# A convolution on TensorE in four 64x64 tiles, and a new order of the steps around it

## The reference

```python
def conformer_conv(a, b, w_dw, b_dw, ln_g, ln_b):      # 512 channels, kernel 31
    u = a * jax.nn.sigmoid(b)
    y = lax.conv_general_dilated(
        u, w_dw[:, None, :], window_strides=(1,), padding=[(CONV_KERNEL - 1, 0)],
        dimension_numbers=('NWC', 'WIO', 'NWC'), feature_group_count=CONV_WIDTH)
    y = layernorm(y + b_dw, ln_g, ln_b)
    return jax.nn.silu(y)

def nsa_mixer(q, k_c, v_c, k_s, v_s, k_w, v_w, gate_logits, positions, ...):
    ...      # three attentions of 8 heads: compressed, selected and window keys
    out = g[..., 0:1] * o_cmp + g[..., 1:2] * o_slc + g[..., 2:3] * o_win

proj = hn @ w_in[l]
...
h = h + jnp.concatenate([y_conv, y_nsa], axis=-1) @ w_out[l]
```

## Time and profile before

| of the profiled execution | |
|---|---|
| span, and time | 1634.1 us; the runs' median is 1633.84 us |
| PE busy | 1572.9 us, 96% |
| PEld busy | 1437.0 us, 88% |
| DVE busy | 1188.7 us, 73% |
| ACT busy | 861.1 us, 53% |
| POOL busy | 351.8 us, 22% |
| chain of waits | PE 80%, DVE 11%, ACT 4%, issue 2%, POOL 1% |
| DMA | 271.15 MB, mean 166 GB/s |

### The profile page before, as it was taken

How to read it: one execution, slowest core, us unless ns; L and a number is a source line. 1 busy time by engine, 2 the same in 40 slices (tenths; PEclk the granted TensorE clock), 3 DMA queues, 4 the chain that set the end, 5 groups by cost and what they waited for, 6 DMA issues and landing times.

```text
span 1634.1 us, 31405 instructions
## 1 busy us (share of the span) xinstructions
PE 1572.9 (96%) x10490; PEld 1437.0 (88%) x10490; DVE 1188.7 (73%) x2258; ACT 861.1 (53%) x1587; POOL 351.8 (22%) x260
## 2 busy tenths in 40 slices
PE   8899998999999999999999999999999999999997
PEld 8789987999887887898999999988888999999996
DVE  3788676788756678455579678779998767776776
ACT  5564445655556643565554555554444545444544
POOL 2344332011000422122048755540000000000000
PEclk9899999999999999999999999999999999999999
DMA  7333244555564720154546644457777665555654
GB/s 268 126 103 104 91 142 155 171 162 180 188 194 126 234 76 1 42 191 142 168 150 203 201 149 145 136 184 241 241 241 227 201 183 190 182 190 183 189 186 148
DMA packets 87848, 271.15 MB, mean 166 GB/s; under 512 B 9824, under 2 KB 26336, under 8 KB 87392
## 3 DMA queue, kind: packets, MB, share of 16 engines
q1 hardware_dynamic: 65088, 237.01, 45.2%
q10 hardware_dynamic: 22688, 33.16, 6.2%
HBM read 258.60 MB, written 11.53 MB: 165 GB/s over the span
## 4 chain that ended last, share of the span: by engine, by line
PE 80%; DVE 11%; ACT 4%; issue 2%; POOL 1%; ACTq 1%; DMA 0%; DVEq 0%; POOLq 0%
PE ps_chunk L488 42%; PE ps_misc L488 21%; PE ps_misc L295 7%; PE ps_chunk L295 4%; PE ps_misc L2457 4%; DVE ffn_arena L1584 1%; DVE w_lo L428 1%; ACT w_hi L421 1%; PE ps_misc L798 1%; DVE mixers_arena L2257 1%; DVE mixers_arena L2258 1%; DVE mixers_arena L2254 1%; PE ps_chunk L495 1%; POOL w_lo L428 1%; DVE mixers_arena L2253 1%
## 5 line engine op out<-in xcount | busy, mean ns | idle before, releaser
L421 ACT ACTIVATE w_hi<-raw 128x512 fp32r<-128x512 f32 (+1 forms) x900 | 548.5, 626 | 495.2 <-PE ps_chunk L488 292.0
L428 DVE TENSOR_TENSOR w_lo<-raw,w_hi 128x512 fp32r<-128x512 f32 x671 | 490.1, 745 | 269.1 <-ACT w_hi L421 259.4
L488 PE MATMUL ps_chunk<-x_hi,w_hi 128*128 128x256 f32 x1792 | 520.0, 290 | 13.6 <-DVE w_lo L428 7.3
L488 PE MATMUL ps_chunk<-x_hi,w_lo 128*128 128x256 f32 x1792 | 508.6, 284 | 0.0
L488 PE MATMUL ps_chunk<-x_lo,w_hi 128*128 128x256 f32 x1792 | 508.3, 284 | 0.0
L428 POOL TENSOR_TENSOR w_lo<-raw,w_hi 128x512 fp32r<-128x512 f32 (+2 forms) x229 | 299.8, 1323 | 539.3 <-ACT w_hi L421 476.0
L488 PEld LDWEIGHTS ps_chunk<-x_hi,w_hi 128*128 128x128 f32 x1792 | 344.8, 192 | 26.1 <-POOL w_lo L428 10.2
L488 PEld LDWEIGHTS ps_chunk<-x_hi,w_lo 128*128 128x128 f32 x1792 | 345.0, 193 | 3.2 <-issue 0.5
L488 PEld LDWEIGHTS ps_chunk<-x_lo,w_hi 128*128 128x128 f32 x1792 | 344.8, 192 | 0.0
L488 PE MATMUL ps_misc<-w_hi,hid_hi 128*128 128x512 f32 x520 | 203.5, 391 | 2.1 <-DVE hid_lo L2536 1.4
L488 PE MATMUL ps_misc<-w_hi,hid_lo 128*128 128x512 f32 x520 | 203.1, 391 | 0.0
(11 more groups left out here) (342 smaller groups left out, 1795.4 us busy)
## 6 DMA issues: line engine op xcount, KB each, us to landing
raw<-in_stream SPq DMA_DIRECT2D x452, 512.0 KB, 3.6
early_rows<-row ACTq DMA_DIRECT2D x64, 128.0 KB, 1.7
row<-early_rows ACTq DMA_DIRECT2D x62, 128.0 KB, 3.2
memory_kv<-mixers_arena ACTq DMA_DIRECT2D x4, 512.0 KB, 5.2
mixers_arena<-in_cmp_w ACTq DMA_DIRECT2D x1, 2048.0 KB, 7.7
mixers_arena<-memory_kv ACTq DMA_DIRECT2D x4, 512.0 KB, 6.3
mixers_arena<-in_consts ACTq DMA_DIRECT2D x1, 1729.0 KB, 7.9
row<-in_rows ACTq DMA_DIRECT2D x3, 512.0 KB, 6.6
```

What stands on the lines that cost most here:

```text
L421: e.activation(w_hi[q % 2][:, s], raw[q][:, s], ACT.Copy).then_inc(made, 1)
L428: e.tensor_tensor(w_lo[q % 2][:, s], raw[q][:, s], w_hi[q % 2][:, s].bitcast(F32), ALU.subtract).then_inc(made, 1)
L488: last = e.matmul(o, stationary[a], moving[b], start=start and i == 0, stop=stop and i == 2, skip_group_check=True)
```

## The change

Three things change, all in the second mixers.

First, the diagonals. A diagonal of 128 channels becomes two of 64x64, each at its own quarter of the array: two groups of channels are taken together (a pair), and for each tap there are four matmuls of 64 rows by 64 columns with 256 time steps, one for each combination of row half and column half. Two of the four write their own half of the channels straight, the other two swapped (row half 0 to column half 1). Each pair takes two PSUM banks, and the strand's bank range grows from two banks (2, 2) to four (0, 4), shared with the dense product. POOL makes one 64-column eye out of the identity and then four builds of 1280 elements instead of eight. The result comes back in eight DVE adds of 64 partitions instead of four of 128.

Second, the DVE taps keep their running sums in Y in SBUF instead of PSUM bank 0, with the bias put in by the first one.

Third, `tile` has a further `yield` behind the turns of the compressed round and behind those of every other round, and MIXERS_2_ORDER is a new string.

```diff
@@ MIXERS_2_ORDER @@
-MIXERS_2_ORDER = ("ddqddddddkddqqddddddddddddddkdddddddddkdddddddqddddddqdddddqqddkddqdqkkkkddqdkdkdddkkccddkdddddddkkk"
...
+MIXERS_2_ORDER = ("ddddddddddddddddkddddddddddddddddddddqdqqdddqdtcdddddddkqdkddddkqdcddkkckkddkqqkkqdkqddcdddddddddddt"
...
@@ the call @@
-            weave(MIXERS_2_ORDER, dense=(0, 4, dense_chunks()), conv=(2, 2, conv), keys=(4, 2, keys()),
+            weave(MIXERS_2_ORDER, dense=(0, 4, dense_chunks()), conv=(0, 4, conv), keys=(4, 2, keys()),
@@ conv_module @@
-            half = CONV_PE // 2
-            diagonals = [cut(half, P), cut(half, P)]
+            half, side = CONV_PE // 2, P // 2
+            block = [slice(0, side), slice(side, P)]
+            diagonals = [cut(2, half, side), cut(2, half, side)]
+            eye = cut(side)
...
-                def diagonal_taps(k, part):
+                def diagonal_taps(pair, part):
                     D_part, lo = diagonals[part], half * part
+                    each = taps[:, 2 * pair:2 * pair + 2, lo:lo + half]
                     return pool.do(lambda e: e.tensor_tensor(
-                        D_part, ident.unsqueeze(1).broadcast_to([P, half, P]),
-                        taps[:, k, lo:lo + half].unsqueeze(2).broadcast_to([P, half, P]), ALU.mult), used_up[part])
+                        D_part, eye.unsqueeze(1).unsqueeze(1).broadcast_to([P, 2, half, side]),
+                        each.unsqueeze(3).broadcast_to([P, 2, half, side]), ALU.mult), used_up[part])
                 yield from evacuated(first)
+                pool.do(lambda e: e.tensor_tensor(eye, ident[:, 0:side], ident[:, side:P], ALU.add))
...
-                for k in range(CONV_T):
-                    at, ps, free = banks.take()
+                for pair in range(CONV_T // 2):
+                    at, ps, free = banks.take(2)
                     for part in range(2):
-                        for some in range(0, half, 2):
-                            for j in range(half * part + some, half * part + some + 2):
-                                used_up[part] = pe.do(mm(ps[:, 0:T], diagonals[part][:, j - half * part, :],
-                                                         U[:, k, j:j + T], j == 0, j == CONV_PE - 1),
-                                                      m[part], made[k // 2], *free)
+                        for some in range(half):
+                            j = half * part + some
+                            for swap in range(2):
+                                for rows in range(2):
+                                    o = ps[block[rows ^ swap], rows * CW:rows * CW + T]
+                                    used_up[part] = pe.do(mm(o, diagonals[part][block[rows], swap, some, :],
+                                                             U[block[rows], 2 * pair + swap, j:j + T], j == 0,
+                                                             j == CONV_PE - 1), m[part], made[1], *free)
                             yield
-                        if k + 1 < CONV_T:
-                            m[part] = diagonal_taps(k + 1, part)
-                    yield
-                    while summed[k] is None:
-                        yield "early"
-                    v = dve.do(lambda e, k=k, ps=ps: e.scalar_tensor_tensor(
-                        out=Y[:, k, :], in0=ps[:, 0:T], scalar=c("conv_dw_b_2", k), in1=Y[:, k, :], op0=ALU.add,
-                        op1=ALU.add), used_up[1], summed[k])
-                    banks.release(at, 1, v)
+                        if pair + 1 < CONV_T // 2:
+                            m[part] = diagonal_taps(pair + 1, part)
+                    for k in (2 * pair, 2 * pair + 1):
+                        yield
+                        while summed[k] is None:
+                            yield "early"
+                        for rows in range(2):
+                            to = Y[block[rows], k, :]
+                            part_of = ps[block[rows ^ (k % 2)], rows * CW:rows * CW + T]
+                            v = dve.do(lambda e, to=to, part_of=part_of: e.tensor_tensor(to, to, part_of, ALU.add),
+                                       used_up[1], summed[k], own=False)
+                    banks.release(at, 2, v)
...
@@ taps_by_dve @@
-                                sums_at[:, k, :], src, tap, None, ALU.mult), made[k // 2], own=False)
+                                Y[:, k, :], src, tap, c("conv_dw_b_2", k), ALU.mult, ALU.add), made[k // 2],
+                                own=False)
                         else:
-                            to = Y if j == CONV_K - 1 else sums_at
-                            sums = dve.do(lambda e, k=k, tap=tap, src=src, to=to: e.scalar_tensor_tensor(
-                                out=to[:, k, :], in0=src, scalar=tap, in1=sums_at[:, k, :], op0=ALU.mult,
-                                op1=ALU.add), before[k], own=False)
+                            sums = dve.do(lambda e, k=k, tap=tap, src=src: e.scalar_tensor_tensor(
+                                out=Y[:, k, :], in0=src, scalar=tap, in1=Y[:, k, :], op0=ALU.mult, op1=ALU.add),
+                                before[k], own=False)
```

More of the change, by code:

```diff
@@ L73 @@
 LAST_QUARTER_LAST = ((0, 0), (0, 1), (1, 0), (1, 1), (0, 2), (1, 2), (0, 3), (1, 3))
-MIXERS_2_ORDER = ("ddqddddddkddqqddddddddddddddkdddddddddkdddddddqddddddqdddddqqddkddqdqkkkkddqdkdkdddkkccddkdddddddkkk"
-                  "ddccttddkdkkqtqdkdddqqkcctttccttkkctttktctttkqqcttkkqtcccttqtttttttqqttkktctttttctttkttttqtttckttqkq"
-                  "tttttttttttttttckccctccttcccctqcckqckcckqccqkccqckckqckcccqqccqkqkccqccccckqccccqkcqckqkqdddqqkkdddd"
-                  "dddddddddddddddddddddddddddddddddddddddddckqt")
+MIXERS_2_ORDER = ("ddddddddddddddddkddddddddddddddddddddqdqqdddqdtcdddddddkqdkddddkqdcddkkckkddkqqkkqdkqddcdddddddddddt"
+                  "dkkdqkkdckddkkdqqdqckkddtkktdcttktdctttqttktcccktqkktttqcttttqccccdkqddtctttdtcqtdttttkttdtddtqcdqtt"
+                  "tttttqtttkktcctccttdddtddtcttddtccqqktccdddkcdtkttttcddqtdtkttccqddccctkqckkqtccqcqcdtqkdddddddkkkdq"
+                  "dccccccqdqkdqkkcqccdcccddddqcccqkqdcckkdcqddq")
 STREAM = {}
```

1 line of the change is left out of this document (removed).

## The result

The changed kernel took 1642.16 us (median of four runs, 1637.83 to 1644.47) against 1632.78 for the kernel before, in the same series. The ratio is 1.0049, with an interval from 1.0029 to 1.0068: slower by 8 us going by the ratio, by 9.4 going by the two medians, where 1629.7 and faster were forecast. It lies outside the range of 1622 to 1636.

A forecast was written before the change was run, and what follows sets the result against it. PE was taken to bound the second mixers, with DVE close behind in the middle and setting its pace afterwards. DVE's timeline -7.4 plus stretches 3.3 gave -4.1: 1634.1 to 1630.0, median 1629.7, range 1622 to 1636 us.

The forecast's parts named there:

- The dense part: Dense product w_in_2 of the second mixers: builds moved ahead of two w_lo taken as 0 us, bounds -3.0 and +3.0.
- the -1.5 at T0: First softmax front of the middle (scores, softmaxes, turns, convolution): 1.5 us earlier, PE having no 8-record block before the first scores.
- Rival C: In the middle's last three steps, two half-clock stretches behind PE's gaps cost 3.4 us: 1633.1, no change; chance 0.21.
- Two fall in the DVE-bound part: In the middle, two of four POOL builds stretch DVE operations, 1.65 us each: 3.3 lost, bounds 0 and 4.7.
- DVE's timeline in the new order: In the middle, DVE's work sets the sum: steps of 15.3, 15.3, 11.4, 10.5 and 7.0 us, -7.4 in all.
- Four at once: Convolution on PE: four quarter records run together, 320 taking 17.7 us, 17.7 less than before.
- Rival D: Convolution on PE: quarters go two by two, costing 35.4 us again; 1637.3, slower by a hair; chance 0.09.
- Bubbles: PE's copy waits in the middle, 6.7 us: new boundaries and order bring -3 in all, bounds -6.7 and +1.
- Rival B: No stretch of taps (-3.3) or the dense part loses its waits (-3.0): some 1626.5, both 1623.4; chance 0.20.

The follow-up runs named there:

- x1: The changed kernel with POOL's eye and first two diagonal builds two w_lo later, PE's order the same: 1633.3 us, ratio 1.0006.
- x6: x1 with ten unread matmuls ahead of the turn with the 4.85 us gap in the middle and four ahead of the next: 1632.5 us, ratio 1.0000.
- x12: x9 with unread matmuls ahead of each turn in the middle for which PE waits in x9's profile: 1628.4 us, ratio 0.9970.
- x9: The changed kernel with four diagonal buffers, all builds in the dense part, and one more step letter for the convolution's strand: 1630.2 us, ratio 0.9980.
- x7: x1 with each of POOL's builds of 1280 elements as four instructions of 320: 1633.4 us, ratio 1.0004.
- x4: The changed kernel with the order string and step boundaries of before, keeping quarters, four banks and SBUF sums: 1637.4 us, ratio 1.0023.
- x10: A second series of x9's program, its intended filling keyed to moved letters so that nothing was filled: 1630.7 us, ratio 0.9991.
- x5: The changed kernel with ten unread matmuls right ahead of the dense-part turn that waits for L1987: 1635.8 us, ratio 1.0012.

## Why the prediction was wrong

- *The dense part: "I take 0, bounds -3.0 and +3.0".* This step failed. It measured +10.0 against before and +11.5 against the -1.5 at T0. The edit was seen ("two builds and an eye move ahead of two w_lo on POOL"), but its price was looked for on POOL's side, in late w_lo. Nobody asked which DVE instructions the builds now stand beside, and what waits for those on PE. The trace before could have led there. It has two builds from 570.98 to 576.20 and beside them the same line of the rotation (L1978 there), 5.39 us for four instructions of 128 columns that take 1.27 in the kernel after; DVE's next w_lo stands behind it, PE waits 1.32 us for that w_lo, and then its records take 0.41 us in place of 0.28, the low clock. DVE's and PE's timeline of before:

```profile
571.61 5.39 DVE L1978 TENSOR_TENSOR mixers_arena<-mixers_arena 128x128 f32<-128x128 f32 x4
577.03 1.25 DVE L1979 TENSOR_TENSOR mixers_arena<-mixers_arena 128x128 f32<-128x128 f32 x1
...
578.53 0.69 DVE L428 TENSOR_TENSOR w_lo<-raw,w_hi 128x512 fp32r<-128x512 f32 x1
...
579.27 0.58 PE L488 MATMUL ps_chunk<-x_hi,w_hi 128*128 128x256 f32 x1 [1.32 <-DVE w_lo L428]
```

  The prediction read only the 1.8 us for POOL's w_lo and left this wait for DVE's out. Of the 10.0, the gap against the old one is 4.43 - 1.32 = 3.1, other waits for w_lo 1.4, the clock 9.4 less the 1.7 lost before = 7.7; the convolution block that is no longer in this part gives back 1.7. That is 10.5, 0.5 more than measured. x1 took all of it away.
- *Rival C, "the gain is given back", 1633.1.* The kind of loss was the right one, a low clock behind PE's waits, with a price of 1.7 us for each stretch, read from the single row of 3.4 us. The stretches of the kernel after were 18.9 and 14.7 us long. The size failed, for the first (9.4 us) by a factor of over five, and with it the range: C was held to be "the same", and it was the case that made the kernel slower. I also put it into the middle alone, where DVE's lead hides most of it (x6: about 1.4 us), and not into the dense part, where PE sets the end and every half-clock microsecond counts.
- *"Two fall in the DVE-bound part: 2 x 1.65 = 3.3".* Two they were; they cost 1.8 and 2.3, 4.1 in all, the upper end of 4.7 being nearer than the value taken.
- *DVE's timeline in the new order.* Right: with stretches and low clock taken away (x12) its five steps are 15.3, 15.4, 11.1, 10.8 and 7.0 against 15.3, 15.3, 11.4, 10.5 and 7.0. (The terms given for the fourth add up to 10.3, not to 10.4; it changes nothing.)
- *Four at once.* Right, 0.058 us a record. Rival D falls. The Trainium skill ("TensorE: Matmul & The Clock Gate", Part 3, The mechanism) has matmuls start and end strictly in the order of issue. What the prediction's rival read out of that, that only two would overlap, does not hold for these records.
- *Bubbles.* Right in kind: copy waits 6.7 to 1.7. But waits of PE for DVE's back halves, 9.6 us, took their place; that was foreseen as idle time, and not as what brings down the clock.
- *Rival B* (no tap is stretched, or the dense part loses its waits) is false in both halves: the taps with their sums in SBUF are held beside a build, where those with sums in PSUM were not (nine in 3.61 us). The Trainium skill ("GPSIMD Engine Reference", section 1, Specifications) has this contention for DVE instructions with two SBUF inputs. L1987 and L1893 are such, and the trace agrees with it for them (5.13 and 3.78 us, against 0.86 and 1.6 alone).

## What to carry to other kernels

When an instruction of one engine moves, look at what it now runs beside (here POOL's builds beside DVE instructions that read SBUF twice), and follow the stretched instruction to whoever waits for it; its own queue is the smaller part of the question. Price a gap of PE not by its length but with the low clock that may follow, first where PE sets the end. And a handwritten order that is consumed step by step must be counted again whenever a strand gets one step more or less.

## What the runs showed of the hardware

- After a gap of 4.43 us PE was granted 1.2 GHz for 18.9 us, though it was busy for all of them; after 1.39 us (x9) for some 14; after 3.44 us (x7) and 1.32 us (before) for some 3.5. In x4 18 us of value products ran so. Yet after 2.56 us (the changed kernel, to 666.82) and 1.71 us (x1, to 578.73) the clock stayed at 1.00. So the length of a gap tells neither whether the clock falls nor for how long, and executions of one program differ. What else decides it is open.
- Filling PE's waits with unread matmuls kept the granted clock at 1.00 (x12, from T1 on), and the middle took 59.6 us against 64.2 and 61.7 in the same program unfilled (x9, x10), although PE had more to do. Filling the one long gap (x5) did not keep the clock up.
- 64x64 quarters in float32: 0.058 us for a record of 256 columns against 0.221 for one on the whole array, a factor of 3.8.
- A 4-column DVE instruction with SBUF operands took 2.3 us beside a POOL build of 2.4, 2.1 more than alone; beside a build in four pieces (x7) it took 0.5 us more than alone, and POOL took up to 1.8 times as long for the build.
